# Short convolution computed inside its input product, and stick-breaking queries and keys produced transposed, with the heads' first two steps in the product's last blocks

## The reference, cut to what matters

```
def stick_breaking_mixer(xn, w_qkv, w_o):
    qkv = (xn @ w_qkv).reshape(b, s, 3, SB_HEADS, SB_HEAD_DIM)
    ...
        z = jnp.einsum('bhqd,bhkd->bhqk', qb, k) * scale
        log_beta = jax.nn.log_sigmoid(z)
        log_1m_beta = jnp.where(mask, jax.nn.log_sigmoid(-z), 0.0)
        suffix = lax.cumsum(log_1m_beta, axis=3, reverse=True) - log_1m_beta
        weights = jnp.where(mask, jnp.exp(log_beta + suffix), 0.0)
        return jnp.einsum('bhqk,bhkd->bhqd', weights, v)
    ...
    return o @ w_o

def short_conv_mixer(xn, w_in, conv_w, w_out):
    b_gate, c_gate, u = jnp.split(xn @ w_in, 3, axis=-1)
    h = c_gate * u
    hp = jnp.pad(h, ((0, 0), (CONV_WIDTH_3 - 1, 0), (0, 0)))
    conv = sum(conv_w[i] * hp[:, i:i + s] for i in range(CONV_WIDTH_3))
    return (b_gate * conv) @ w_out
```

## Time and profile before

| what | value |
|---|---|
| median of 3 runs | 3207.89 us |
| the profiled execution's own time | 3203.6 us |
| span of its records | 3201.8 us |
| TensorE busy | 2853.4 us, 89% |
| VectorE busy | 1926.7 us, 60% |
| ScalarE busy | 1211.6 us, 38% |
| mean granted TensorE clock | 0.934 of full speed |

### The profile page before, as it was taken

One profiled execution on the slowest core, in us unless ns is written; L12 is line 12 of the kernel. 1 busy time (PEld: TensorE's weight loads), 2 busy tenths in 40 slices (PEclk: granted clock), 3 DMA queues, 4 the chain that ended last, 5 costly groups with the idle time before them and its releaser, 6 DMA issues.

```text
span 3201.8 us, 44221 instructions
## 1 busy us (share of the span) xinstructions
PE 2853.4 (89%) x17644; PEld 2532.1 (79%) x17644; DVE 1926.7 (60%) x2106; ACT 1211.6 (38%) x1438; POOL 570.1 (18%) x469
## 2 busy tenths in 40 slices
PE   8995799999969979986589899997999848999999
PEld 7985689999858879975489778986898747987898
DVE  7965266688758875544455556555655456555654
ACT  4333144333334334333233344333433424334532
POOL 6921120058325830001000000000000020000000
PEclk9997599999989999999689999998999868999999
DMA  7743015557416745432135344435443404435342
GB/s 263 285 158 108 28 59 206 190 205 272 158 53 236 275 161 193 179 116 64 50 148 191 135 133 177 184 119 163 179 188 125 145 0 175 188 114 173 140 195 105
DMA packets 127213, 499.46 MB, mean 156 GB/s; under 512 B 11984, under 2 KB 13296, under 8 KB 93712
## 3 DMA queue, kind: packets, MB, share of 16 engines
q1 hardware_dynamic: 113824, 450.46, 38.6%
q0 software_dynamic: 13296, 47.74, 4.4%
HBM read 497.11 MB, written 1.05 MB: 156 GB/s over the span
## 4 chain that ended last, share of the span: by engine, by line
PE 67%; DVE 14%; issue 10%; ACT 4%; POOL 3%; DMA 2%; DVEq 0%; SPq 0%; POOLq 0%; ACTq 0%
PE duo L940 9%; PE duo L941 8%; PE duo L942 8%; PE duo L1234 6%; PE duo L997 5%; PE duo L1235 5%; PE duo L1236 5%; PE duo L998 5%; PE duo L999 5%; DVE down_lo L330 2%; DVE in_lo L330 2%; ACT in_hi L323 2%; DVE hid_hi L1097 1%; POOL arena L1593 1%; DMA ring_in<-in_ffn_in 1%
## 5 line engine op out<-in xcount | busy, mean ns | idle before, releaser
L330 DVE TENSOR_TENSOR in_lo<-ring_in,in_hi 128x2048 fp32r<-128x2048 f32 x299 | 714.2, 2389 | 335.6 <-ACT in_hi L323 335.4
L940 PE MATMUL duo<-feat_hi,in_hi 128*128 128x256 f32 x3136 | 889.9, 284 | 12.5 <-DVE in_lo L330 6.3
L941 PE MATMUL duo<-feat_lo,in_hi 128*128 128x256 f32 x3136 | 886.2, 283 | 0.0
L942 PE MATMUL duo<-feat_hi,in_lo 128*128 128x256 f32 x3136 | 885.6, 282 | 0.0
L323 ACT CAST in_hi<-ring_in 128x2048 fp32r<-128x2048 f32 x302 | 574.7, 1903 | 358.1 <-PE duo L1236 308.6
L940 PEld LDWEIGHTS duo<-feat_hi,in_hi 128*128 128x128 f32 x3136 | 600.8, 192 | 25.7 <-DVE in_lo L330 6.6
L941 PEld LDWEIGHTS duo<-feat_lo,in_hi 128*128 128x128 f32 x3136 | 602.1, 192 | 7.3
L942 PEld LDWEIGHTS duo<-feat_hi,in_lo 128*128 128x128 f32 x3136 | 601.5, 192 | 0.0
L330 DVE TENSOR_TENSOR down_lo<-ring_down,down_hi 128x1024 fp32r<-128x1024 f32 (+1 forms) x196 | 375.3, 1915 | 142.3 <-ACT down_hi L323 142.3
L997 PE MATMUL duo<-down_hi,hid_hi 128*128 128x512 f32 x1040 | 413.2, 397 | 10.4 <-DVE hid_lo L1099 10.2
L998 PE MATMUL duo<-down_lo,hid_hi 128*128 128x512 f32 x1040 | 410.4, 395 | 0.0
(11 more groups left out here) (325 smaller groups left out, 2897.9 us busy)
## 6 DMA issues: line engine op xcount, KB each, us to landing
ring_in<-in_ffn_in SPq DMA_DIRECT2D x196, 1024.0 KB, 6.5
ring_down<-in_ffn_down SPq DMA_DIRECT2D x132, 512.0 KB, 3.5
ring_down<-in_ffn_down SPq DMA_DIRECT2D x64, 1024.0 KB, 4.8
mod_w<-in_w_ada POOLq DMA_DIRECT2D x72, 512.0 KB, 5.3
ring_in<-in_sb_w_qkv SPq DMA_DIRECT2D x24, 1024.0 KB, 5.1
ring_in<-in_conv_w_in SPq DMA_DIRECT2D x12, 1024.0 KB, 5.1
ring_in<-in_gla_w_in SPq DMA_DIRECT2D x12, 1024.0 KB, 5.1
ring_in<-in_nsa_w_in SPq DMA_DIRECT2D x10, 1024.0 KB, 5.2
```

Of the source, the lines that this page charges most:

```text
L330: dve.tensor_tensor(lo[:, s, 0:n], raw[:, s, 0:n], hi[:, s, 0:n].bitcast(F32), ALU.subtract).then_inc(lo_ready.sem, 1)
L940: pe.matmul(out, hi, self.feat_hi[:, c, :], start=opens, stop=False, skip_group_check=True)
L941: pe.matmul(out, hi, self.feat_lo[:, c, :], start=False, stop=False, skip_group_check=True)
L942: return pe.matmul(out, lo, self.feat_hi[:, c, :], start=False, stop=(c == KC - 1), skip_group_check=True)
```

## The change

The two stick-breaking layers lose `Turn` and get a new product, `QkvIn`. It takes the blocks in the order values, values, then queries low half, keys low half, queries high half, keys high half. The four blocks of queries and keys (b = 2 to 5) are computed with the roles exchanged: 128 columns of the weights are stationary and the 256 tokens move, so that they come out with features on the partitions. For that a unit takes 48 multiplications of 256 columns instead of 24 of 512. Since 1/rms now lies along the free axis, it is first spread over the partitions (two VectorE instructions of 128x128, two TensorE multiplications behind block 0, one ScalarE copy), and VectorE multiplies it in when it reads the result (two instructions of 128x512 for a block; ScalarE reads nothing there). Behind the first unit of blocks 4 and 5 stand the steps 0 and 1 of `StickBreaking` on TensorE; their parts on the other engines stand in the same blocks. `StickBreaking` itself starts at step 2. The second unit of the output product (`late`) is no longer split in the product's last block but in step 4 of `StickBreaking`.

The short convolution becomes one product, `ConvIn`, with the blocks in the order c low, u low, c high, u high, b low, b high, and a small stage `ConvFeed`. VectorE multiplies c by u while it reads u. Behind the first unit of blocks 2 and 4 TensorE transposes half of c*u (8 transposes), behind that of block 5 the low half of b; the taps follow on ScalarE (the first) and VectorE (the two others) straight from PSUM; the gating and the split into high and low parts come chunk by chunk after the last unit's split. The last 8 transposes stand within the first unit of the output product, which waits for its features chunk by chunk.

```
+    EARLY, LATE = 2, 4
...
+    def scalar(self, act):
+        for step in range(self.EARLY, self.n + 3):
+            self.step_scalar(act, step)
+            if step == self.LATE:
+                in_hi(self.k, act, self.late)
...
+            self.step_vector(dve, step)
+            if step == self.LATE:
+                in_lo(self.k, dve, self.late)
...
+class QkvIn(Linear):
...
+    ORDER = [2 * D, 2 * D + BLK, 0, D, BLK, D + BLK]
...
+                for c in range(4):
+                    f_hi, f_lo = self.feat_hi[:, 4 * h + c, :], self.feat_lo[:, 4 * h + c, :]
+                    pe.matmul(out, w_hi[:, c, mine], f_hi, start=h == 0 and c == 0 and j % 2 == 0, stop=False, skip_group_check=True)
+                    pe.matmul(out, w_hi[:, c, mine], f_lo, start=False, stop=False, skip_group_check=True)
+                    last = pe.matmul(out, w_lo[:, c, mine], f_hi, start=False, stop=h == 1 and c == 3 and j % 2 == 1, skip_group_check=True)
+                if h == 1 and j == 1:
+                    last.then_inc(k.acc_ready.sem, 1)
+            last.then_inc(k.in_used.sem, 1)
+            if h == 0 and b >= 4:
+                if b == 4:
+                    pe.wait_ge(k.sb_consts.sem, self.sb.c0 + 2)
+                    pe.wait_ge(k.acc_read_dve.sem, self.rd0 + 6)
+                self.sb.step_tensor(pe, b - 4)
...
+        for b, (lo, hi) in enumerate(self.blocks):
+            if b >= 4:
+                self.sb.magnitude(dve, b - 4)
+            in_lo(k, dve, self.u0 + 2 * b + 2)
+            if b < 2:
+                self.wait_acc(dve, 1, b)
+                dve.tensor_scalar(self.dst[:, 1, lo:hi], self.acc(1, b), self.feeds.rstd(1), None, ALU.mult).then_inc(k.acc_read_dve.sem, 1)
+            else:
+                if b == 2:
+                    dve.wait_ge(k.rrow_ready.sem, self.rr0 + 1)
+                rows = self.rrow.unsqueeze(1).broadcast_to([P, 2, TOKENS])
+                for i in range(2):
+                    c = lo // P + 2 * i
+                    self.wait_acc(dve, i, b)
+                    dve.scalar_tensor_tensor(self.qk[:, c:c + 2, :], k.bank_tiles(4 + b % 2 * 2 + i), HEAD ** -0.5 if lo < D else 1.0, rows,
+                                             ALU.mult, ALU.mult).then_inc(k.acc_read_dve.sem, 1)
+            if b == 4:
+                self.sb.softplus(dve, 0)
+            if b < 5:
+                in_lo(k, dve, self.u0 + 2 * b + 3)
...
+class ConvIn(Linear):
...
+    ORDER = [D, 2 * D, D + BLK, 2 * D + BLK, 0, BLK]
...
+    def mid(self, pe, b):
+        k = self.k
+        if b in (2, 4):
+            half = b // 4
+            pe.wait_ge(k.acc_read_dve.sem, self.rd0 + 3 * half + 3)
+            self.turn_half(pe, half, lambda t, c: k.y[:, t, c * P:(c + 1) * P])
+        if b == 5:
+            pe.wait_ge(k.conv_tap.sem, self.p0 + KC)
+            pe.wait_ge(k.acc_read_act.sem, self.ra0 + 3)
+            pe.wait_ge(k.acc_read_dve.sem, self.rd0 + 7)
+            self.turn_half(pe, 0, lambda t, c: k.proj[:, t, c * P:(c + 1) * P])
+    def turn_half(self, pe, half, src):
+        for c in range(4 * half, 4 * half + 4):
+            for t in range(TT):
+                last = pe.transpose(self.home(c)[:, t * P:(t + 1) * P], src(t, c), self.k.c("ident"))
+            last.then_inc(self.k.turned.sem, 1)
...
+            if b in (1, 3):
+                half = b // 2
+                dve.wait_ge(k.acc_read_act.sem, self.ra0 + half + 1)
+                dve.wait_ge(k.acc_read_dve.sem, self.rd0 + 3 * half + 1)
+                for t in range(TT):
+                    self.wait_acc(dve, t, b)
+                    dve.scalar_tensor_tensor(k.y[:, t, part_of(half)], self.acc(t, b), self.feeds.rstd(t), self.dst[:, t, lo - D:hi - D],
+                                             ALU.mult, ALU.mult).then_inc(k.acc_read_dve.sem, 1)
+            else:
+                self.wait_acc(dve, 1, b)
+                dve.tensor_scalar(self.dst[:, 1, lo:hi], self.acc(1, b), self.feeds.rstd(1), None, ALU.mult).then_inc(k.acc_read_dve.sem, 1)
+            in_lo(k, dve, self.u0 + 2 * b + 3)
+            if b in (2, 4):
+                self._later_taps(dve, b // 4)
+        self.feature_lo(dve, 0)
...
+                out = self.taps[:, c, back:n]
+                dve.scalar_tensor_tensor(out, self.home(c)[:, 0:n - back], k.col(f"conv_w_3_{tap}", c), out,
+                                         ALU.mult, ALU.add).then_inc(k.conv_tap.sem, 1)
...
+        dve.wait_ge(k.conv_tap.sem, self.p0 + KC * (half + 1))
+        for i in range(5):
+            if i < 4:
+                c = mine[i]
+                dve.wait_ge(k.turned.sem, self.t0 + KC + c // 2 * 2 + 2)
+                dve.tensor_tensor(gated(c), gated(c), self.home(c), ALU.mult).then_inc(k.conv_gated.sem, 1)
+            if i:
+                c = mine[i - 1]
+                dve.wait_ge(k.turn_hi.sem, self.h0 + c + 1)
+                dve.tensor_tensor(k.feat2_lo[:, c, :], gated(c), k.feat2_hi[:, c, :].bitcast(F32), ALU.subtract).then_inc(k.turn_lo.sem, 1)
...
+    def turn(self, pe, half):
+        self.feeds.turn_last(pe)
+    def scalar(self, act):
+        self.feeds.feature_hi(act, 1)
     def vector(self, dve):
-        k, n = self.k, TOKENS
-        wait_all(dve, self.before)
-
-        for c in range(KC):
-            last = dve.tensor_scalar(self.acc[:, c, :], self.hT[:, c, :], k.col("conv_w_3_2", c), None, ALU.mult)
-        k.dve_link(dve, last)
-        for tap, back in ((1, 1), (0, 2)):
-            for c in range(KC):
-                acc = self.acc[:, c, back:n]
-                last = dve.scalar_tensor_tensor(acc, self.hT[:, c, 0:n - back], k.col(f"conv_w_3_{tap}", c), acc, ALU.mult, ALU.add)
-            k.dve_link(dve, last)
-        k.dve_link(dve, dve.tensor_tensor(self.acc[:], self.acc[:], self.bT, ALU.mult))
-        feat_from(k, dve, self.acc[:], 0, KC).then_inc(k.conv_done.sem, 1)
+        self.feeds.feature_lo(dve, 1)
...
-    proj = Linear(k, before, w_qkv, "store", dst=k.proj)
     qk = heads_view(k, 0, 16)
-    turn = Turn(k, proj, lambda t, c: k.proj[:, t, c * P:(c + 1) * P], qk, 16,
-                scale=lambda c: HEAD ** -0.5 if c < KC else 1.0)
+    proj = QkvIn(k, before, w_qkv, qk)
     rows = lambda h: slice((h % 2) * HEAD, (h % 2 + 1) * HEAD)
-    att = StickBreaking(k, turn, lambda h: qk[rows(h), h // 2, :], lambda h: qk[rows(h), KC + h // 2, :],
+    att = StickBreaking(k, proj, lambda h: qk[rows(h), h // 2, :], lambda h: qk[rows(h), KC + h // 2, :],
                         lambda h, t: k.proj[:, t, 2 * D + h * HEAD:2 * D + (h + 1) * HEAD], 16 * TOKENS)
-    return [proj, turn, att, Linear(k, att, w_o, "norm")]
+    return [proj, att, Linear(k, att, w_o, "norm")]
...
-    proj = Linear(k, before, "conv_w_in_3", "store", dst=k.proj)
-    prod = Product(k, proj, lambda t: k.y[:, t, :], lambda t: k.proj[:, t, D:2 * D], lambda t: k.proj[:, t, 2 * D:3 * D])
-    bh = heads_view(k, 0, 16)
-    turn = Turn(k, prod, lambda t, c: k.proj[:, t, c * P:(c + 1) * P] if c < KC else k.y[:, t, (c - KC) * P:(c - KC + 1) * P], bh, 16)
-    conv = ShortConv(k, turn, bh[:, 0:KC, :], bh[:, KC:16, :], 16 * TOKENS)
-    return [proj, prod, turn, conv, Linear(k, conv, "conv_w_out_3", "norm")]
+    proj = ConvIn(k, before, "conv_w_in_3")
+    feed = ConvFeed(k, proj)
+    return [proj, feed, Linear(k, feed, "conv_w_out_3", "norm")]
```

329 lines of the change are left out of this document (237 added, 92 removed).

## The result

The changed kernel takes 3187.81 us (median of 5 runs, 3179.33 to 3190.27) where the kernel before, run beside it, takes 3204.56 (5 runs, 3202.24 to 3209.92). The ratio is 0.9935, 95% interval 0.9918 to 0.9952. So the change takes 14 to 21 us off by the ratios (0.44 to 0.65%), 16.8 and 13.8 us by the medians of the two sets; forecast were 23.6 less than 3207.9, that is 3184.3, in a range of 3172 to 3195. The likeliest case came about: faster, at a time 3.5 us above the one that was said.

A forecast was written before the change was run, and what follows sets the result against it. TensorE bounds the kernel, with holes at three places; 19.1 (convolution) + 4.2 + 3.3 (stick-breaking) - 3.0 (slow clock) = 23.6 us less: 3180.0 for the profiled execution, plus 4.3 for the median 3184.3, 8-in-10 range 3172 to 3195.

The forecast's parts named there:

- The likeliest case: Whole kernel: the forecast itself, 3184.3 us, as a case of 3180 to 3188 us with chance 0.52.
- Convolution, 19.1 forecast: Layer 1 before the output product: 28.2 us shrink to 5.8, less 3.2 for transposes and 0.1 for chunks.
- the convolution keeps a hole: Rival, layer 1: serial gating chain, low clock and splits over 1 us late leave 3196 us; chance 0.08.
- Stick-breaking, 2.7 forecast for layer 0 with the slow clock, 1.8 for layer 3: Stick-breaking layers: 4.2 us gained in layer 0, 3.3 in layer 3, less 1.5 each for the slow clock.
- the spread of 1/rms: Stick-breaking input product: two 128x128 TensorE multiplications cost 0.5 us a layer, the rest runs beside block 1.
- the late split: Stick-breaking step 4: cast and split between ln and softplus of pair 4 idle TensorE 4.15 us a layer.
- The slow clock behind it: Behind step 4's idle TensorE runs near half clock: 1.5 us for each stick-breaking layer, bounds 0 and 3.4.
- the late split is hidden: Rival, stick-breaking step 4: no bubble and no slow clock, 11.3 us more gained, 3173 us; chance 0.12.
- stick-breaking gives nothing: Rival, stick-breaking layers: two slow stretches and late splits in blocks 4 and 5, 5.8 us less gained, 3190; chance 0.16.
- Narrow multiplications: Stick-breaking queries and keys: 48 of 256 columns take 5.75 us, not 5.44, costing 2.5 us over 8 units.
- Slower, the ring starves: Rival, 24 units of the input products: late VectorE splits make TensorE wait 1.4 us each, 3217 us; chance 0.03.
- the sign of being wrong that the prediction named: Input products: TensorE idle released by `in_lo` inside them would show the prediction wrong.

The follow-up runs named there:

- the two sets: Changed kernel beside the kernel before, measured twice without edit: 3187.81 us, ratio 0.9935, then 3191.34 us, ratio 0.9956.
- experiment 2: Changed kernel with the split of the output product's second unit moved from step 4 of stick-breaking to step 8: 3174.25 us, ratio 0.9901 to the kernel before.
- Experiment 7: Changed stick-breaking layers with the short convolution of the kernel before: 3204.36 us, ratio 0.9990 to the kernel before.
- experiment 3: Changed kernel with the split of the output product's second unit in step 7 in place of step 4: 3185.48 us, ratio 0.9952 to the kernel before.
- the two answers here: Two separate edits of the changed kernel: late split to step 8, 3174.25 us; convolution's low-half gating and parts ahead of the last block's store and split, 3177.28 us.
- the kernel with both: Changed kernel with late split in step 8 and the convolution's low-half gating and parts earlier: 3164.25 us, ratio 0.9871 to the kernel before.

## Why the prediction was right, and where its 3.5 us went

- **Convolution, 19.1 forecast: 18.3 in the profiled execution, 16.9 to 19.2 over the seven with the same instructions there.** The time from the end of the input product to the output product fell from 28.2 to 5.69 us, by 22.5 (22.4 forecast), a group of transposes 0.79 (0.8), the taps 3.21 (3.3), and they delay nothing. Rival "the convolution keeps a hole" asked for gating in series and splits late by over 1 us; the idle would then be longer than 5.8 and idle released by `in_lo` would stand in the product; neither is there.
- **Stick-breaking, 2.7 forecast for layer 0 with the slow clock, 1.8 for layer 3: 2.36 and 2.14.** Its terms, read singly in layer 0: a narrow unit lasts 5.76 us (5.75), so 0.32 more a unit (0.31); step 0 lengthens its unit by 1.29, step 1 by 3.0 (the product's last multiplication ends at 1899.14, 8.69 after the cast at 1890.45; in a bare unit, 1871.88 to 1877.27 + 0.28, that is 5.67), together 4.3 (4.5); the spread of 1/rms 0.37 (0.5); the late split 3.94 of idle (4.15). The slow clock behind it was sized too low: 1.5 us for each layer, where experiment 2 shows 2.3 in layer 0 and 1.7 in layer 3. Layer 3 took 138.3 to 138.4 us in all four executions with these instructions, 2.1 to 2.2 less than before; layer 0 took 144.7 in two of them and 146.5 in the two whose input product starts with more of the slow clock, so its gain is 0.5 to 2.4 us, and 2.36 is at the upper end. Rival "the late split is hidden" was wrong for this order and right for another: it needed step 8 (experiment 2). Rival "stick-breaking gives nothing" had the right bubble and two slow stretches behind each, which would leave -1.3 of the 4.5 us. On the clock layer 0 lies between the two (2.3 us; 1.5 in the forecast, 3.4 in the rival); its other term, a late split in blocks 4 and 5, cost nothing, since no unit of the product waits. Experiment 7 measured 3.2 us with an interval from no change to 6.4, nearer the forecast; its stages alone gave 2.4 + 2.2 = 4.6, and FFN 0 and FFN 3 behind them took 1.2 and 1.1 back.
- **Narrow multiplications.** 48 in 5.76 us are 120 ns each, as the earlier trace rows had them at another place in the program; the row held and the price of 2.5 us a layer with it. An estimate by the formula that the Trainium skill ("TensorE: Matmul & The Clock Gate", Back-to-back issue gap) gives for the isolated case is 109.2 ns; no row here shows that for multiplications of 256 columns.
- **Slower, the ring starves:** no. In the whole input product of layer 0, and in those of layers 1 and 3 behind the start of their second unit, TensorE's timeline has no idle of over 0.3 us in the changed kernel, let alone one released by `in_lo`. The one wait for `in_lo` stands ahead of that second unit, 1.07 us in layer 1, and the kernel before has it too, with 1.04: it is not the sign of being wrong that the prediction named.
- **What failed: the sum took every other stage as unchanged.** The same instructions took 4.65 us more (the ledger). Over the ten executions that I have of other kernels than before these five stages took 0.0 to 4.6 us more than in the one execution of the kernel before, 2.7 on average; how much of that the change brings isn't shown. Where it was looked at it is the clock, and mostly behind an idle that both kernels have (3.65 of the 4.65 us are in FFN 0, 1 and 3): where a stage starts TensorE waits 3.3 us for VectorE. The windows view over the first 7 us of FFN 0 and FFN 1, in the kernel before:

```profile
1957.78:1961.28 3.50, 3.50 (x16) 0.54 0.51 213
1961.28:1964.78 3.50, 3.50 (x31) 0.98 0.00 0
2271.57:2275.07 3.50, 3.43 (x16) 0.57 0.48 204
2275.07:2278.57 3.50, 3.50 (x31) 0.94 0.02 5
```

and in the changed one:

```profile
1960.17:1963.67 3.50, 3.50 (x15) 0.50 0.48 201
1963.67:1967.17 3.50, 3.50 (x21) 0.64 0.00 0
2256.82:2260.32 3.50, 3.50 (x15) 0.50 0.46 192
2260.32:2263.82 3.50, 3.50 (x20) 0.59 0.00 0
```

The slow stretch lasts about 3.6 us in the one and some 6 in the other, which is 10 multiplications fewer in the second window, 1.2 us a stage. The prediction priced the slow clock only where it saw a new idle. It should have carried a term for the old ones, a few microseconds wide.
- **The rest is the yardstick.** I went from the profiled execution (3203.6) to the median of the runs (3207.9) by adding 4.3 us. Beside the changed kernel the kernel before had 3204.56, and in the other sets 3203.3 to 3207.5. With 23.6 off 3204.56 the forecast would have been 3181, and 6.8 us too low. The gain was overstated by 6.8 us (9.8 in the second set), and that the time came out within 3.5 us is in part luck: the 4.3 us added for the yardstick happened to go the other way.

**What stays open** is what makes a slow stretch long or short. It is not the change alone: FFN 0 had 188.18 us in one execution of the changed kernel and 189.41 in another. FFN 1 had 188.25 and 188.19 in the two executions with the old convolution, and 188.7 to 189.5 in eight of the nine with the new one; in the ninth (experiment 3) it had 188.16, but mixer 1 was 1.5 us longer there than after (108.73 against 107.27), so that the two together came out the same, 296.9 against 296.8 after. No kernel was made that changes only this. The Trainium skill ("TensorE: Matmul & The Clock Gate", Part 1: The HAM clock gate) reports that the number of slow multiplications at a kernel's start varies between runs of one kernel. The two values of FFN 0 show the same in the middle of a kernel. The Trainium skill puts it down to where the clock's own measuring stands when the kernel starts; no row here shows that, and a forecast can't know it.

## What to carry to other kernels

When an instruction is moved to a quieter time, look in program order at what stands next behind it on each in-order engine, not at how idle the engine is: VectorE idles 40% of this program, and a 2.3-us split set between ln and softplus cost TensorE 3.94 us of idle and some 2 of slow clock, while behind the last low part it cost none. A term of the sum for a removed hole is safe (5.69 for 5.8); a total of many stages carries besides a few microseconds of clock that can't be put down to the edit, so compare stage by stage, and more than one execution: one stage differed by 1.8 us between two executions of one kernel. And after a change ask of each idle that remains whether what it waits for needs it: the two answers here were worth about as much as the change itself. In stages they gave 19.8 us and the change 22.8; in totals the kernel with both is 41 us under the kernel before, the changed kernel 14 in the same set and 17 in the first.
